# First attention's gated outputs turned by VectorE and ScalarE inside the gate chunks, three quarters of them, instead of by TensorE

## What is computed

```python
def mixer_a(h, w_in, w_out):
    q, k, v, g = jnp.split(h @ w_in, 4, axis=-1)
    heads = lambda t: t.reshape(b, s, SB_HEADS, SB_HEAD_DIM)
    o = stick_breaking_attention(heads(q), heads(k), heads(v)).reshape(b, s, SB_WIDTH)
    return (o * jax.nn.silu(g)) @ w_out
```

## Time and profile before

| what | value |
|---|---|
| median of 3 runs | 2073.56 us (2071.52 to 2074.47) |
| the profiled execution | 2074.44 us, its span 2072.7 us |
| TensorE (PE) busy | 2060.4 us, 99% of the span |
| VectorE (DVE) busy | 1285.6 us, 62% |
| ScalarE (ACT) busy | 1084.7 us, 52% |
| GpSimd (POOL) busy | 6.1 us |
| mean granted TensorE clock | 0.999 |
| read from HBM | 371.64 MB, 180 GB/s over the span |

### The profile page before, as it was taken

The page is one execution under the profiler, slowest core; times in us unless marked ns, Lnnn a source line. Parts: engine busy times, 40 slices in busy tenths (PEclk is TensorE's granted clock), DMA queues, the critical chain, the costliest instruction groups (busy, mean ns, idle before and its releaser), DMA issues.

```text
span 2072.7 us, 27180 instructions
## 1 busy us (share of the span) xinstructions
PE 2060.4 (99%) x10784; PEld 1761.4 (85%) x10784; DVE 1285.6 (62%) x1656; ACT 1084.7 (52%) x1539; POOL 6.1 (0%) x12
## 2 busy tenths in 40 slices
PE   9999999999999999999999999999999999999998
PEld 8888888888898888888889988888888888888886
DVE  5555556556877677657955566866546555655554
ACT  6444566645566677546564345554434434434444
POOL 0000000000000000000000000000000000000000
PEclk9999999999999999999999999999999999999999
DMA  7666655665555555565645456666666666666664
GB/s 258 187 187 191 175 151 150 191 189 184 182 178 187 170 146 163 178 196 179 193 147 162 128 147 206 193 191 187 193 192 190 193 193 184 193 193 190 191 192 147
DMA packets 211101, 375.43 MB, mean 181 GB/s; under 512 B 13843, under 2 KB 48885, under 8 KB 210454
## 3 DMA queue, kind: packets, MB, share of 16 engines
q1 hardware_dynamic: 210982, 373.79, 59.7%
HBM read 371.64 MB, written 2.10 MB: 180 GB/s over the span
## 4 chain that ended last, share of the span: by engine, by line
PE 98%; DMA 1%; ACT 1%; DVE 0%; issue 0%; SPq 0%; ACTq 0%
PE acc L521 19%; PE acc L523 19%; PE acc L522 19%; PE acc L1052 6%; PE acc L618 3%; PE xb L1052 3%; PE tp L1052 3%; PE acc L1055 3%; PE acc L945 2%; PE acc L946 2%; PE acc L947 2%; PE tp L533 2%; PE tp L618 1%; PE xb L618 1%; PE acc L621 1%; PE tp L1055 1%
## 5 line engine op out<-in xcount | busy, mean ns | idle before, releaser
L1647 DVE TENSOR_TENSOR wlo<-raw,whi 128x1024 fp32r<-128x1024 f32 x634 | 773.7, 1224 | 622.9 <-ACT whi L1113 621.1
L1113 ACT ACTIVATE whi<-raw 128x1024 fp32r<-128x1024 f32 x634 | 670.3, 1059 | 772.4 <-PE acc L523 449.6
L521 PE MATMUL acc<-whi,ahi 128*128 128x512 f32 (+1 forms) x976 | 376.8, 386 | 0.1
L523 PE MATMUL acc<-whi,alo 128*128 128x512 f32 (+1 forms) x976 | 374.0, 383 | 0.0
L522 PE MATMUL acc<-wlo,ahi 128*128 128x512 f32 (+1 forms) x976 | 373.8, 383 | 0.0
L521 PEld LDWEIGHTS acc<-whi,ahi 128*128 128x128 f32 x976 | 183.2, 188 | 37.6 <-issue 2.7
L523 PEld LDWEIGHTS acc<-whi,alo 128*128 128x128 f32 x976 | 183.2, 188 | 36.2
L522 PEld LDWEIGHTS acc<-wlo,ahi 128*128 128x128 f32 x976 | 183.3, 188 | 34.2
L1052 PE MATMUL acc<-bT,whi 128*128 128x512 f32 x512 | 160.8, 395 | 0.0
L521 PE MATMUL acc<-whi,bhi 128*128 128x512 f32 x384 | 150.2, 391 | 0.0
L523 PE MATMUL acc<-whi,blo 128*128 128x512 f32 x384 | 149.5, 389 | 0.0
(11 more groups left out here) (382 smaller groups left out, 3150.0 us busy)
## 6 DMA issues: line engine op xcount, KB each, us to landing
raw<-in_mlp_w SPq DMA_DIRECT2D x256, 512.0 KB, 4.2
raw<-in_w_in_a SPq DMA_DIRECT2D x128, 512.0 KB, 4.2
raw<-in_w_ple_gate SPq DMA_DIRECT2D x64, 512.0 KB, 4.3
raw<-in_w_in SPq DMA_DIRECT2D x64, 512.0 KB, 3.8
raw<-in_w_in_b SPq DMA_DIRECT2D x40, 512.0 KB, 4.1
raw<-in_w_out_a SPq DMA_DIRECT2D x32, 512.0 KB, 4.2
raw<-in_w_out_b SPq DMA_DIRECT2D x32, 512.0 KB, 4.3
raw<-in_w_out SPq DMA_DIRECT2D x32, 512.0 KB, 4.6
```

The source lines that it names most:

```text
L521: pe.matmul(o, hi[:, kt, tok], whi[:, slot, wc], start=start, stop=False)
L523: mm = pe.matmul(o, lo[:, kt, tok], whi[:, slot, wc], start=False, stop=stop)
L1113: act.activation(whi[:, u % RING, 0:n], raw[:, u % RING, 0:n], ACT.Copy).then_inc(hi_done, 1)
L1647: dve.tensor_tensor(wlo[:, u % RING, 0:n], raw[:, u % RING, 0:n], whi[:, u % RING, 0:n].bitcast(F32), ALU.subtract).then_inc(lo_done, 1)
```

## The change

For ogA's first three chunks (features 0 to 1535) the turning goes to VectorE and ScalarE, chunk j-1 within gate chunk j. At the end of g0, g1 and g2, behind `gated`, VectorE waits for its own result and transposes all 32x32 blocks of the chunk in place of their block, back into `stg` (`flipped`, two instructions of 128x512). In the chunk that follows ScalarE copies two of the four feature bands from there to their partitions (`bands_moved`, hooks 1 and 2, four copies of 32x256 each), VectorE turns the other two straight from `nat` (hooks 3 and 4, four block transposes each), and at hook 6 ScalarE rounds (`hi_moved`) and VectorE forms the remainder (`lo_moved`). Six of TensorE's eight batches go away with their evacuations (L1151, L1684); batches 6 and 7 stay where they were. No transfer is added, removed or moved.

```diff
-TURNED_BY = {"x2": "gate0", "x4": "gate1", "x5": "out2"}
-MOVED = [(name, c) for name in TURNED_BY for c in range(3)]
+FLIPPED = [("ogA", 0), ("ogA", 1), ("ogA", 2)]
+MOVED = [(name, c) for name, cs in (("ogA", [0, 1, 2]), ("x2", [0, 1, 2]), ("x4", [0, 1, 2]), ("x5", [0, 1, 2])) for c in cs]
-OG_EARLY, OG_LATE = {6: [0, 1]}, {0: [2, 3], 2: [4, 5], 4: [6, 7]}
+OG_LATE = {"ogA": {4: [6, 7]}, "ogB": {0: [2, 3], 2: [4, 5], 4: [6, 7]}}
...
 # TensorE, stage g
-                    hooks = join(hooks, {6: [lambda: pe.wait_ge(sem("attA_o"), HEADS // 2)]}, turns("ogA", OG_EARLY))
+                    hooks = join(hooks, {6: [lambda: pe.wait_ge(sem("attA_o"), HEADS // 2)]})
...
 # ScalarE
+            def bands_moved(name, c, q, par):
+                if q == 0:
+                    act.wait_ge(sem("flipped"), FLIPPED.index((name, c)) + 1)
+                    if MOVED.index((name, c)):
+                        act.wait_ge(sem("split_lo"), MOVED.index((name, c)))
+                blocks = stg[:, par].rearrange("p t (f j b) -> p t f j b", f=QT, j=P // BLK)
+                for i in range(P // BLK):
+                    m = act.activation(mov[q * BLK:(q + 1) * BLK, :, i], blocks[i * BLK:(i + 1) * BLK, :, :, q, :], ACT.Copy)
+                m.then_inc(sem("moved"), 1)
...
+            def og_moved(c):
+                def halves():
+                    act.wait_ge(sem("attA_logits"), 2 * c + 2)
+                    hi_moved("ogA", c, bhi)
+                par = (S["g"].c0 + c) % 2
+                return {1: [lambda: bands_moved("ogA", c, 0, par)], 2: [lambda: bands_moved("ogA", c, 1, par)], 6: [halves]}
...
-                along(s, j, join(attention_of(3 + j), his("ogA", bhi, None, OG_EARLY) if j == 3 else {}))
+                along(s, j, join(attention_of(3 + j), og_moved(j - 1) if j else {}))
...
 # VectorE
+            def flipped(src, c, par):
+                for t in range(TT):
+                    m = dve.transpose(stg[:, par, t, :], src[:, t, c * CH:(c + 1) * CH])
+                m.then_inc(sem("flipped"), 1)
...
+            def og_moved(c):
+                return {3: [lambda: blocks_turned("ogA", c, 2)], 4: [lambda: blocks_turned("ogA", c, 3)],
+                        6: [lambda: lo_moved("ogA", c, bhi, blo)]}
...
-                along(s, j, ahead=softplus_of(3 + j), hooks=join(attention_of(3 + j), los("ogA", bhi, blo, None, OG_EARLY) if j == 3 else {}))
+                along(s, j, ahead=softplus_of(3 + j), hooks=join(attention_of(3 + j), og_moved(j - 1) if j else {}))
                 gated(s.c0 + j, (s.c0 + j) % 2, j, sem("attA_o"), 2 * (j + 1))
+                if j < 3:
+                    dve.wait_ge(evac_dve, s.c0 + j + 1)
+                    flipped(nat, j, (s.c0 + j) % 2)
```

More of the change, by code:

```diff
@@ L293, in build @@
         x_done = sem("x_done")
-        order = [("gcol", 1), ("x0", 8), ("p", 2), ("norms", 1), ("ogA", 8), ("x1", 8), ("x2", [6, 7]), ("ckv", 2), ("kr", 1),
+        order = [("gcol", 1), ("x0", 8), ("p", 2), ("norms", 1), ("ogA", [6, 7]), ("x1", 8), ("x2", [6, 7]), ("ckv", 2), ("kr", 1),
                  ("cq", 2), ("ogB", 8), ("x3", 8), ("meta", 1),
@@ L722, in post @@
                 for j in range(4):
-                    product(S[f"out_{ab}"], j, bhi, blo, need=y if j == 0 else None, free=gates_out if layer and j == 0 else None, hooks=turns(y, OG_LATE) if j == 0 else {})
+                    product(S[f"out_{ab}"], j, bhi, blo, need=y if j == 0 else None, free=gates_out if layer and j == 0 else None, hooks=turns(y, OG_LATE[y]) if j == 0 else {})
                 for j in range(4):
@@ L1322, in post @@
                     p = (s.c0 + j) % 2
-                    along(s, j, his(y, bhi, None, OG_LATE) if j == 0 else {})
+                    along(s, j, his(y, bhi, None, OG_LATE[y]) if j == 0 else {})
                     ended(s, j)
@@ L1690, in lo_batch @@
                 m.then_inc(tp_done, 1)
+            def flipped(src, c, par):
+                for t in range(TT):
+                    m = dve.transpose(stg[:, par, t, :], src[:, t, c * CH:(c + 1) * CH])
+                m.then_inc(sem("flipped"), 1)
             def blocks_turned(name, c, q):
+                src = nat if name == "ogA" else x
                 if q == 0:
@@ L1697, in blocks_turned @@
                     m = dve.transpose(mov[q * BLK:(q + 1) * BLK, :, i],
-                                      x[i * BLK:(i + 1) * BLK, :, c * CH:(c + 1) * CH].rearrange("p t (f j b) -> p t f j b", f=QT, j=P // BLK)[:, :, :, q, :])
+                                      src[i * BLK:(i + 1) * BLK, :, c * CH:(c + 1) * CH].rearrange("p t (f j b) -> p t f j b", f=QT, j=P // BLK)[:, :, :, q, :])
                 m.then_inc(sem("moved"), 1)
@@ L1895, in post @@
                     p = (s.c0 + j) % 2
-                    along(s, j, los(y, bhi, blo, None, OG_LATE) if j == 0 else {})
+                    along(s, j, los(y, bhi, blo, None, OG_LATE[y]) if j == 0 else {})
                     ended(s, j)
```

## The result

The changed kernel takes 2079.97 us (median of 12 runs, 2077.58 to 2083.22) against 2073.57 us for the kernel before in the same rounds (2071.52 to 2076.4): a ratio of 1.0031, 95% interval 1.0024 to 1.0038, or 6.4 us slower. The profiled execution's span is 2079.3 us, 6.6 us longer. The forecast was 6.7 us slower, 2080.3 us.

The account below looks back on a forecast made before the run. TensorE, busy 99% of the span, was taken to bound the kernel. Removal -2.6 us plus stalls +9.35 gave +6.7 on the median 2073.56, so 2080.3 us; own range 2077.3 to 2082.7, stated range 2075.5 to 2085.5.

Parts of the forecast that it names:

- The removal: g3 and out_a: three pairs of transpose batches leave TensorE, 0.88 us each, 2.6 us saved.
- The prices: Added VectorE and ScalarE work: flip 1.5 us with its wait, bands 1.7, blocks 1.79 per hook, rounding 1.0.
- my ends: Low and high costs: flip 1.0 to 1.9 us, bands 1.2 to 2.1; net +3.7 to +9.1 us.
- The chain: g1 to g3: added work ahead of VectorE's values copy makes it and the splits late, 6.7 growing to 11.5 us.
- The stalls one by one: TensorE waits at g1's sums 2.5 us, g2's unit 1.5, g2's sums 2.7, g3's sums 2.65.
- last lateness less last margin: g3's sums: lateness 11.5 us minus 2.15 to spare, equal to all stalls together, 9.35 us.
- the one that had TensorE at full speed between the stalls: g1 to g3: TensorE's own lateness was taken as only its earlier stalls, 2.5, then 4.0, then 6.7 us.
- the signs I had named: TensorE idle 2 to 3 us at sums in g1, g2, g3, once before g2's unit; clock under 1.00 meant wrong.
- the wait for `wlo` in g2: TensorE idle ahead of a unit's first matmul in g2, waiting for a split, 1.5 us.
- The clock rival: Stalls in g set off half-speed matmuls, about 2.2 us a fall: 2082.5 us with one, 2089.1 with four; chance 0.10.
- The hidden case: Added work in g fits the other engines' idle time, no stalls: 2070.9 us; chance 0.08.

Follow-up runs that it names:

- nothing turned: Changed kernel with ogA's first three chunks turned by no engine; out_a reads the turned x instead: 2071.19 us, ratio 0.9989 to the kernel before.
- filled run: Changed kernel plus 14 idle TensorE transposes ahead of each of the three sums it waits at: 2079.38 us, ratio 1.0028 to the kernel before.
- copy-first: Changed kernel with VectorE's copy of the attention's values put ahead of the split of the same step: 2083.24 us, ratio 1.0043 to the kernel before.
- no-bands: Changed kernel without ScalarE's 24 band copies, those features left zero: 2078.85 us, ratio 1.0020 to the kernel before.
- the second six: Changed kernel measured once more, unaltered, for another execution's trace: 2081.15 us, ratio 1.0034 to the kernel before.
- its filled version: Kernel with the values copy ahead of the split, plus 24 idle TensorE transposes ahead of g3's sums alone: 2079.66 us, ratio 1.0030.
- flips twice: Changed kernel with each flip at the end of g0, g1 and g2 done twice: 2084.98 us, ratio 1.0056 to the kernel before.
- the fastest version: Changed kernel's instructions at other steps, values copy ahead of the split, one more VectorE wait: 2070.39 us, ratio 0.9984 to the kernel before.

## Why the prediction was right

- *The removal*: 0.88 us a pair, 2.6 in all. The run with nothing turned shows 2.7 by E.
- *The prices*: two flips take 1.30 us (128x512 in 0.69, overlapping), I took 1.44; bands 1.68 to 1.70, taken 1.7; blocks 1.79; rounding 1.04. The estimate for the flip from a copy of the same width was 0.14 high, far inside my ends.
- *The chain*: lateness 6.7, 7.3, 9.0, 11.5 us forecast, 6.5, 7.0, 8.5, 11.0 measured. The flips' 0.14 us too much, three times over, is most of the difference.
- *The stalls one by one*: 2.5, 1.5, 2.7, 2.65 forecast; 2.3, none, 2.2, 1.1 measured. The sum I gave, last lateness less last margin, 11.5 - 2.15 = 9.35, held (9.0 us lost), but not its split. The step that failed is the one that had TensorE at full speed between the stalls. At half speed for 3.4 us it came to the unit in g2 late enough (4.0 us instead of 2.5) to find its split done, and to the last sums 7.9 us late instead of 6.7; the copy there was 0.4 us less late than forecast, which makes the rest of the missing 1.6 us. Of the signs I had named, three did not come as the forecast had them: the granted clock fell in g, the wait for `wlo` in g2 was missing, and the last stall was 1.1 us instead of 2 to 3.
- *The clock rival* had a chance of 0.10 and a wrong price. Its premise came true, two falls, but I had added 2.2 us a fall to the stalls. The filled run shows that a fall ahead of a later wait costs nothing here, the copy-first pair that one behind the last wait costs its 1.6 us. That none came behind the last stall of the changed kernel was luck: with one, as in the no-bands and the copy-first run, the time would have been about 1.6 us longer, still inside the range. The changed kernel's spread from run to run (5.6 us, against 4.9 before) goes in part with the clock: the slowest of its 12 runs, 2083.22 us, is the only one at 0.996, and the fastest of the second six, 2077.45 us, the only one at 0.998. The Trainium skill (TensorE: Matmul & The Clock Gate, Why this matters for your kernels) warns of long gaps between bursts; the trace agrees in kind, 1.2 GHz behind a gap of 2.2 us, though the gap in the copy-first run's g2, 2.3 us of waiting, had none behind it.
- *The hidden case* rested on totals of idle time and on the rule that occupancy is a fine measure for the other engines (the Trainium skill, Trainium Kernel Development and Optimization, Best Practices). Neither engine was near its limit, and the kernel was 6.4 us slower. The totals did say that room exists: the same instructions, moved, fit in it.

## What to carry to other kernels

When a saturated engine is relieved by two that have time to spare, do not add up their idle time; write down each place where the saturated one needs them next, its margin there (here 4.2, 3.3, 2.3 and 2.15 us), and what the new work puts in front of it. Work put behind the last need is free, the same work ahead of it costs its full length less the margin. Lateness is carried on, so several stalls on one chain cost the last lateness less the last margin, however they are split; what a lower clock takes comes on top only behind the last wait (1.6 us in the copy-first run). And before a difference of 1 or 2 us in medians is read, look through the whole trace for such a fall elsewhere.

## What was not expected of the hardware

- In the traces with a stall in g, 12 idle gaps of TensorE ahead of a stalled matmul were longer than 2 us (2.07 to 3.89). Nine had a fall to 1.2 GHz beside them, for 3.4 us each, beginning between 0.2 us ahead of the restart and 1.7 us behind it. Three had none: 2.33 us in g2 of the copy-first run, 2.38 at the same place of its filled version, 2.22 in g3 of the run with flips twice. The gaps of 0.8 to 1.4 us had none either. What tells the gaps just above 2 us apart was not found.
- Idle time is not needed for a fall: the one near 1070 us came in 7 of 13 traces with no gap ahead of it, behind six matmuls of 33 rows that start about 0.5 us apart.
- With transposes into a free bank while waiting, the clock stayed at 2.4 GHz (1.00 in every window of g, with 14 or 24 of them).
- Four 32x256 copies of ScalarE to other partitions take 0.42 us each with no overlap, and four such transposes of VectorE 0.45; but two 128x512 transposes within their partitions overlap by 0.08 us, 1.30 for two of 0.69.
- In ckv, 200 us behind the change, TensorE waits 0.2 to 1.0 us for a remainder of x2 (L1702) in both traces of the changed kernel and in those of six others, the fastest version's among them, and not in the kernel before nor in four others. In the changed kernel ScalarE waited there 2.59 us for a load of w_dkv, 1.59 in the kernel before. Why that load lands later was left open.
